# Second feed-forward of a hybrid block: up products of 20 tiles in pairs with seven block products for eight

## The chip, the cores and the metric

One core of a Trainium2 chip runs the kernel in one launch. The metric is the device time of an execution in microseconds. TensorE (PE) does the matmuls, VectorE (DVE) and ScalarE (ACT) the arithmetic on tiles, GpSimd (POOL) prepares weights, and SyncE (SP) issues the weight loads.

## The reference

What is computed, with one layer, 1024 tokens, a width of 1024 and D_FF = 2816, all in float32:

```python
def swiglu(h, w1, w3, w2):
    return (jax.nn.silu(h @ w1) * (h @ w3)) @ w2

def reference(...):
    ...
        h = modulate(rms_norm(x, g_ffn1[l]), sh1, sc1)
        x = x + 0.5 * gt1[:, None, :] * swiglu(h, w1_a[l], w3_a[l], w2_a[l])
        h = modulate(rms_norm(x, g_mix[l]), sh2, sc2)
        x = x + gt2[:, None, :] * hybrid_mixer(...)
        h = modulate(rms_norm(x, g_ffn2[l]), sh3, sc3)
        x = x + 0.5 * gt3[:, None, :] * swiglu(h, w1_b[l], w3_b[l], w2_b[l])
    return rms_norm(x, g_final)
```

The change is in the last `swiglu` alone, and in the order and the tiles of the norm ahead of it.

## The kernel before

Everything is held transposed: channels on the 128 partitions, the 1024 tokens along a row. A width of 1024 is 8 k tiles, D_FF is 22 f tiles. PSUM is four units of 128x1024 (`unit_a` to `unit_d`), each of two banks of 512 tokens.

**Split operands.** A float32 product is made of three fp32r matmuls, high by high, high by low and low by high (`product`, L486): each operand is split in a high part (a rounding copy) and a low part (the rest). One slab is one weight tile column, 8 k tiles of 128x128; a product of a slab with all tokens is 8 k tiles x 3 parts x 2 halves = 48 matmuls of 128x512. POOL splits the weights, half a slab (4 k tiles, 128x512) at a time: L456 makes `w_high`, L458 `w_low`. Two slabs of split weights are held, four of unsplit ones (`raw`), which SP loads ahead.

**Feed-forward.** The 22 f tiles go in chunks of 8, 8 and 6 (`CHUNKS`). `up`: the slab of w1 into unit_a, that of w3 into unit_b; ACT takes silu of unit_a (L840), DVE multiplies by unit_b (L1153), ACT makes `g_high` (L842) and DVE `g_low` (L1155). `down`, after each chunk: 8 output tiles, in unit_c and unit_d by turns, of 8 or 6 k tiles each; DVE adds each into the residual `x_res` (L1174). The very first pair of slabs (`first_pair`, L565) goes half by half of the tokens, k by k, right behind the norm; DVE makes the norm's `xr` (L1105) and `h_low` (L1113), ACT what is between (L830, L832). The last down chunk (`last_down`) is followed tile by tile by the end of the kernel: DVE scales with the final gain (L1187), PE transposes (L629), ACT squares (L776), DVE sums the squares (L1050).

The order on each engine is as written; engines meet by counting semaphores, and a wait holds up all that is behind it on its engine.

```python
for part in range(2):
    ...
    pool.wait_ge((slab_half, slab_used)[part], 4 * i + r - 1)
    high = w_high[:, r % 2, rows, :]
    pool.tensor_tensor(high, raw[:, r, rows, :], one, ALU.mult).then_inc(high_split, 1)
    pool.wait_ge(high_split, 2 * (4 * i + r) + part + 1)
    pool.tensor_tensor(w_low[:, r % 2, rows, :], raw[:, r, rows, :], high.bitcast(F32),
                       ALU.subtract).then_inc(slab_split, 1)
```

Of the kernel before, what the change touches and what calls it, by code (L numbers as in the profile page):

```python
# [30 lines left out]
P = 128  # L31
# [26 lines left out]
def phases():  # L58
# [17 lines left out]
    ffn("ffn2", False)  # L76
    out.append(("end", 0, (0, 0, 0, 0), 0, 0))
    return out

# [53 lines left out]
def block_kernel(nc, a, out):  # L133
    at = starts()
    with ExitStack() as ctx:
# [27 lines left out]

        x_rows = sb("x_rows", [P, J, D], rH)
# [34 lines left out]
        y_gain = sb("y_gain", [P, 2, T], rA)  # L199
        rms = sb("rms", [P, J], rA + 8 * KB)  # L200
# [108 lines left out]
        stored = sem("stored")  # L309
        act_step = sem("act_step")  # L310
        dve_step = sem("dve_step")

        block = ctx.enter_context(nc.Block())


        @block.sync
        def _(sp):
# [106 lines left out]
            ffn("ffn2", a["w1_b"][0], a["w3_b"][0], a["w2_b"][0], False)  # L424
# [12 lines left out]
        def _(pool):  # L437
# [24 lines left out]
            with pool.Fori(1, at["end"].slab // 4) as i:  # L462
                split(i, False)


        @block.tensor
        def _(pe):
# [164 lines left out]
            def last_down(i, count):  # L632

                here = at["ffn2.down2"]
                for e in range(2):
                    slab(here.slab + 2 * i + e, e, C_ + e, here.unit[C_ + e] + i, g_high, g_low, count,
                         (g_ready, here.g - count))
                    if e == 1:
                        back(2 * i, i, 0)
                    elif not isinstance(i, int):  # L640
                        back(2 * i - 1, i - 1, 1)

            def ffn(name, with_ada):
                for n, (_, count) in enumerate(CHUNKS):
# [4 lines left out]
                    if name == "ffn2" and n == 2:  # L649
                        last_down(0, count)  # L650
                        with pe.Fori(1, KD // 2) as i:
                            last_down(i, count)
                        back(KD - 1, KD // 2 - 1, 1)
                    else:
                        downs(f"{name}.down{n}", count, 1 if n == 2 else None)
# [96 lines left out]
            ffn("ffn2", False)  # L752
# [13 lines left out]
        def _(act):  # L766
# [36 lines left out]
            def norm(n, h0):  # L803
# [14 lines left out]
                for step in range(2 * KD):  # L818
# [4 lines left out]
                    half, m = divmod(step, KD)  # L823
                    t = slice(HALF * half, HALF * half + HALF)
                    tile = xr[n][:, step % 4, :]
# [6 lines left out]
                    act.activation(h_high[:, m, t], tile, ACT.Copy).then_inc(h_split, 1)  # L832
# [176 lines left out]
            norm(2, at["norm2"].h)  # L1009
            for n in range(3):  # L1010
                up("ffn2", n)
            here, ends = at["ffn2.down2"], at["end"]
            with act.Fori(0, KD // 2) as i:
                for e in range(2):
                    m = 2 * i + e
# [513 lines left out]
```

## Time and profile before

| | us |
|---|---|
| median of 3 executions (2393.04 to 2394.76) | 2393.91 |
| span of the profiled execution (first to last instruction) | 2389.7 |
| PE busy in it | 2308.2 (97%) |
| POOL busy in it | 1100.9 (46%) |
| DVE, ACT busy in it | 909.8 (38%), 320.6 (13%) |
| second feed-forward, from the first matmul to the last down tile | 1639.7 to 2369.2 |

The profiled execution has no time of its own beside its span; the span is 4.2 us under the median, which is taken as what lies around it. Times inside the profile are counted from its start. PE's busy time is drawn from modelled ends of pipelined matmuls, so the pace of a stretch is better read from the chain that ended last, where each piece is a run of matmuls with its length.

### The profile page before, as it was taken

The numbers are of one execution on the slowest core, as the hardware profiler recorded it, in microseconds if no ns is written. First come the engines' busy times: TensorE is split into PE (matmuls) and PEld (weight loads), VectorE is DVE, ScalarE is ACT, GpSimd is POOL, SyncE is SP. The second block draws the span as 40 slices with busy tenths as digits, with TensorE's granted clock in tenths as the row PEclk, the third lists the DMA queues.
The fourth block names the chain that finished last, engine by engine and source line by source line (L and its number), as shares of the span: only waits on it lengthen the run. The fifth ranks groups of instructions, "written<-read, shape, count | busy, mean of one in ns | idle before, by whom it ended". The sixth has DMA issues, their size and how long they took to land.

```text
span 2389.7 us, 27721 instructions
## 1 busy us (share of the span) xinstructions
PE 2308.2 (97%) x10370; PEld 1898.9 (79%) x10370; DVE 909.8 (38%) x1219; ACT 320.6 (13%) x372; POOL 1100.9 (46%) x824
## 2 busy tenths in 40 slices
PE   5899999999999899999999989999999999999997
PEld 4788788878888678888888867887888888888886
DVE  6645124331012699475665544436011101110134
ACT  3311000000011331010101121115110001000112
POOL 3354444444445453444444455543544444444452
PEclk8999999999999999999999999999999999999998
DMA  7344124321121332223222144411111111111111
GB/s 282 106 147 133 44 85 117 114 79 47 50 47 50 115 97 75 84 80 88 84 75 88 53 167 132 137 47 36 53 49 48 48 49 47 50 46 51 41 39 70
DMA packets 258446, 194.29 MB, mean 81 GB/s; under 512 B 21524, under 2 KB 238752, under 8 KB 257248
## 3 DMA queue, kind: packets, MB, share of 16 engines
q1 hardware_dynamic: 234752, 154.52, 21.3%
q10 hardware_dynamic: 23648, 39.20, 5.2%
q8 instruction: 24, 0.39, 0.1%
q14 instruction: 22, 0.18, 0.0%
HBM read 167.34 MB, written 25.17 MB: 81 GB/s over the span
## 4 chain that ended last, share of the span: by engine, by line
PE 93%; DVE 3%; ACT 1%; SPq 1%; issue 0%; DMA 0%; POOL 0%; DVEq 0%; POOLq 0%; ACTq 0%
PE unit_a L486 32%; PE unit_b L486 31%; PE unit_c L486 12%; PE unit_d L486 12%; PE unit_d L726 1%; PE unit_a L565 1%; SPq L340 1%; PE unit_b L565 1%; DVE xr L1105 1%; PE unit_c L609 1%; DVE rstd L1062 1%; PE unit_c L711 1%; PE unit_d L701 1%; PE unit_d L724 1%; PE unit_c L522 0%
## 5 line engine op out<-in xcount | busy, mean ns | idle before, releaser
L456 POOL TENSOR_TENSOR w_high<-raw,ones 128x512 fp32r<-128x512 f32 x408 | 545.3, 1336 | 1220.1 <-PE unit_b L486 395.7
L458 POOL TENSOR_TENSOR w_low<-raw,w_high 128x512 fp32r<-128x512 f32 x408 | 555.8, 1362 | 32.0
L486 PE MATMUL unit_a<-h_high,w_high 128*128 128x512 f32 x1072 | 333.7, 393 | 6.0 <-POOL w_low L458 4.7
L486 PE MATMUL unit_a<-h_low,w_high 128*128 128x512 f32 x1072 | 331.2, 390 | 0.0
L486 PE MATMUL unit_a<-h_high,w_low 128*128 128x512 f32 x1072 | 331.0, 390 | 0.0
L486 PE MATMUL unit_b<-h_high,w_high 128*128 128x512 f32 x1072 | 330.5, 389 | 0.0
L486 PE MATMUL unit_b<-h_high,w_low 128*128 128x512 f32 x1072 | 330.1, 389 | 0.0
L486 PE MATMUL unit_b<-h_low,w_high 128*128 128x512 f32 x1072 | 330.0, 389 | 0.0
L1153 DVE TENSOR_TENSOR s<-s,unit_b 128x1024 f32<-128x1024 f32 x44 | 53.7, 1221 | 655.5 <-PE unit_b L486 652.9
L486 PEld LDWEIGHTS unit_a<-h_high,w_high 128*128 128x128 f32 x1072 | 200.6, 189 | 48.4 <-POOL w_low L458 5.1
L486 PEld LDWEIGHTS unit_a<-h_low,w_high 128*128 128x128 f32 x1072 | 202.0, 188 | 42.5
L486 PEld LDWEIGHTS unit_a<-h_high,w_low 128*128 128x128 f32 x1072 | 201.8, 188 | 42.4
L486 PEld LDWEIGHTS unit_b<-h_low,w_high 128*128 128x128 f32 x1072 | 201.2, 188 | 41.9
L486 PEld LDWEIGHTS unit_b<-h_high,w_low 128*128 128x128 f32 x1072 | 201.2, 188 | 41.8
L486 PEld LDWEIGHTS unit_b<-h_high,w_high 128*128 128x128 f32 x1072 | 200.9, 188 | 42.0
L840 ACT ACTIVATE s<-unit_a 128x1024 f32<-128x1024 f32 x44 | 45.3, 1029 | 717.5 <-PE unit_a L486 712.6
L486 PE MATMUL unit_c<-g_high,w_high 128*128 128x512 f32 x388 | 121.0, 393 | 7.3 <-DVE mod L1160 7.3
L486 PE MATMUL unit_c<-g_low,w_high 128*128 128x512 f32 x388 | 120.7, 393 | 0.0
L486 PE MATMUL unit_c<-g_high,w_low 128*128 128x512 f32 x388 | 120.4, 392 | 0.0
L486 PE MATMUL unit_d<-g_high,w_high 128*128 128x512 f32 x388 | 119.7, 390 | 0.0
L486 PE MATMUL unit_d<-g_low,w_high 128*128 128x512 f32 x388 | 119.5, 389 | 0.0
L486 PE MATMUL unit_d<-g_high,w_low 128*128 128x512 f32 x388 | 119.5, 389 | 0.0
(233 smaller groups left out, 2266.0 us busy)
## 6 DMA issues: line engine op xcount, KB each, us to landing
raw<-in_w_a SPq DMA_DIRECT2D x60, 512.0 KB, 4.1
raw<-in_w_b SPq DMA_DIRECT2D x60, 512.0 KB, 3.8
raw<-in_w_in SPq DMA_DIRECT2D x44, 512.0 KB, 3.9
ada_raw<-in_w_ada SPq DMA_DIRECT2D x8, 2048.0 KB, 7.9
ada_raw<-in_w_ada SPq DMA_DIRECT2D x8, 1536.0 KB, 7.0
ada_first<-in_w_ada SPq DMA_DIRECT2D x8, 1024.0 KB, 14.2
sg_kept<-s ACTq DMA_DIRECT2D x16, 512.0 KB, 2.6
s<-sg_kept ACTq DMA_DIRECT2D x16, 512.0 KB, 3.3
```

The source lines that it names most:

```text
L340: sp.dma_start(raw[:, r, :, :], w.rearrange("(k p) (f n) -> p k f n", p=P, n=P)[:, :, 0, :]).then_inc(slab_loaded[r], 16)
L456: pool.tensor_tensor(high, raw[:, r, rows, :], one, ALU.mult).then_inc(high_split, 1)
L458: pool.tensor_tensor(w_low[:, r % 2, rows, :], raw[:, r, rows, :], high.bitcast(F32), ALU.subtract).then_inc(slab_split, 1)
L486: last = pe.matmul(unit[u][:, t], w, x[:, k, t], start=(k == 0 and part == 0), stop=(k == kts - 1 and part == 2))
L565: last = pe.matmul(unit[u][:, t], w, x[:, k, t], start=(k == 0 and part == 0), stop=(k == KD - 1 and part == 2))
L609: last = pe.matmul(unit[u][:, t], w, x[:, k, t], start=(k == 0 and part == 0), stop=(k == kts - 1 and part == 2))
L701: last = pe.matmul(unit[D_][0:H, col:col + P], b_now[rows, kk, part, :], ca[rows, kk, part, 0:8, :].rearrange("p d h -> p (d h)"), start=( ...
L711: last = pe.matmul(unit[C_][NS * g2:NS * g2 + NS, col:col + P], xt[:, kk, part, NS * g2:NS * g2 + NS], u_chunk[:, 2 * kk + g2, :], start=T ...
L724: pe.matmul(dst, toep[:, 4 * g2 + kk, :], u_chunk[:, 2 * kk + g2, :], start=True, stop=False)
L726: last = pe.matmul(dst, ca[rows, kk, part, 1:9, :].rearrange("p d h -> p (d h)"), sc_b[rows, kk, part, PAD:], start=False, stop=(part == 1))
L840: act.activation(s0[:, :], unit[A_][:, :], ACT.Silu).then_inc(unit_free[A_], 1)
L1153: dve.tensor_tensor(s1[:, :], s0[:, :], unit[B_][:, :], mul).then_inc(unit_free[B_], 1)
```

## The change

The first two f tiles are done as whole tiles, as before. The other 20 go in 10 pairs of f tiles, two pairs to a chunk, so five chunks. For a pair, w1 (and then w3) is a matrix of 2x2 blocks: rows are the two f tiles, columns the two halves of the 8 k tiles; the activations are 2x2 blocks too: halves of the k tiles by halves of the tokens. The product is made by the Winograd form of Strassen's method: seven block products, each of 4 k tiles x 3 parts = 12 matmuls of 128x512, in place of eight (a tile pair took 2 x 48 = 96 matmuls for a matrix, now 84). For this

- the four activation sums t1 to t4 (each 128x2048) are made once, by DVE, and split by ACT and DVE;
- each matrix needs four sums of weight blocks (128x512), made by POOL, and seven operands split: the high parts now by ACT, the low parts by POOL; `w_high` and `w_low` are a ring of four operands of 4 k tiles;
- the partial results of the four banks are put together by ACT (one copy) and DVE (adds), then silu, product and split of the result block by block: 128x512.

The down products come in six parts: two f tiles after the first pair's first matrix, then four f tiles after each chunk, 8 output tiles each time.

```diff
+PRODUCTS = (("a11", "b11", 0, True), ("s2", "t2", 1, True), ("s1", "t1", 2, True), ("s3", "t3", 3, True),
+            ("a12", "b21", 0, False), ("s4", "b22", 2, False), ("a22", "t4", 3, False))
...
 (POOL)
+            for o in range(8):
+                z, part = divmod(o, 2)
+                pool.wait_ge(w_loaded[z], 16)
+                if o < 4:
+                    pool.wait_ge((slab_half, slab_used)[part], s0_ - 1 + z)
+                else:
+                    pool.wait_ge(operand_used, o - 3)
+                whole(*operand(o % 4), o, raw[:, z, part * HK:(part + 1) * HK, :], one)
...
+            def matrix(here, n):
...
+                def low(q):
+                    pool.wait_ge(operand_high, N7 * m + q + 1)
+                    high, low_ = operand((RING[n] + q) % 4)
+                    pool.tensor_tensor(low_, weight_plain(PRODUCTS[q][0], slots), high.bitcast(F32),
+                                       ALU.subtract).then_inc(operand_low, 1)
+                    pool.wait_ge(operand_low, o + q + 1)
+
+                mixed = w_mixed[:, :, :]
+                summed(a_["a21"], a_["a11"], a_["a21"], ALU.subtract, 1)
+                summed(mixed, a_["a22"], a_["a21"], ALU.subtract, 2)
+                low(0)
+                summed(a_["a11"], mixed, a_["a11"], ALU.add, 3)
+                low(1)
+                summed(mixed, a_["a12"], mixed, ALU.subtract, 4)
+                for q in range(2, N7):
+                    low(q)
...
 (PE)
+            def tile_down(here, m):
...
+                take(C_ + e, at["ffn2"].unit[C_ + e] + here.uses + m // 2)
+                if m < 2:
+                    pe.wait_ge(evacuated, 14 * here.pair[1] + (10, 13)[e])
...
+            def whole_tiles():
...
+                    for n, k in enumerate((range(KD), SECOND_ORDER)[half]):
...
+                                if half == 1 and n == KD - 1 and (u, part) in ((A_, 1), (A_, 2), (B_, 1), (B_, 2)):
+                                    last.then_inc(operand_used, 1)
+                for e in range(2):
+                    take(C_ + e, here.unit[C_ + e])
+                    for k in range(KD):
+                        if k % HK == 0:
+                            pe.wait_ge(operand_low, 4 + 2 * e + k // HK + 1)
...
+            def banks_free(here, n):
+                pair = here.pair[n // 2]
+                if n % 2 == 1 and n // 2 == 0:
+                    for u in (C_, D_):
+                        take(u, at["ffn2"].unit[u] + here.uses)
...
+            def matrix(here, n):
...
+                banks_free(here, n)
+                for q, (_, b_name, to, anew) in enumerate(PRODUCTS):
+                    pe.wait_ge(operand_low, o + q + 1)
+                    if isinstance(o, int) and o == 8 and q in (1, 2, 3, 6):
+                        pe.wait_ge(act_sum_low, {1: 1, 2: 2, 3: 3, 6: 4}[q])
+                    if not anew and to == 0:
+                        pe.wait_ge(first_copied, here.matrix[n] + 1)
+                    elif not anew:
+                        pe.wait_ge(evacuated, done + to)
+                    wh, wl = operand((RING[n] + q) % 4)
+                    bh, bl = act_operand[b_name]
+                    for k in range(HK):
+                        for part, (w_, x) in enumerate(((wh, bh), (wh, bl), (wl, bh))):
+                            last = pe.matmul(bank(w, to), w_[:, k, :], x[:, k, :], ...)
+                    last.then_inc(operand_used, 1)
...
+            def fast_ffn():
+                whole_tiles()
+                here = Chunk(1)
+                matrix(here, 0)
+                first_down()
+                for n in range(1, 4):
+                    matrix(here, n)
+                for m in range(KD):
+                    tile_down(here, m)
+                with pe.Fori(2, PAIRED) as c:
...
-            ffn("ffn2", False)
+            fast_ffn()
...
 (ACT)
+            def weight_high(here, n, q):
...
+                act.wait_ge(operand_used, here.op[n] + q - 3)
+                act.activation(operand((RING[n] + q) % 4)[0], weight_plain(PRODUCTS[q][0], slots),
+                               ACT.Copy).then_inc(operand_high, 1)
...
 (DVE)
+            def act_sums():
+                plain = {name: x[:, :, :] for name, x in act_plain.items()}
+                for n, (to, x, y) in enumerate((("t1", "t3", "t1"), ("t3", "t2", "t3"), ("t2", "t2", "t1"), ("t4", "t4", "t2"))):
+                    dve.tensor_tensor(plain[to], plain[x], plain[y], sub).then_inc(act_sum, 1)
+                    dve.wait_ge(act_sum, n + 1)
...
+            act_sums()
+            sum_low("t2", 1)
+            sum_low("t1", 2)
+            sum_low("t3", 3)
+            whole_product(0)
+            sum_low("t4", 4)
+            whole_product(1)
```

In each matrix DVE adds a bank into an SBUF block five times; after the second matrix of a pair it also multiplies four blocks (one straight from PSUM, three with both factors in SBUF) and makes four low parts (both inputs in SBUF).

Three places in the order. **DVE, behind the norm ahead of the second feed-forward.** Before:

```order
L1113 TENSOR_TENSOR h_low<-xr_69,h_high 128x512 [waits h_split] x3
L1145 UNCONDITIONAL_BRANCH [waits h_ready]
L1145 ISA
L1152 ISA [waits unit_free_a]
L1153 TENSOR_TENSOR s_58<-s_57,unit_b 128x1024 [waits slab_used]
L1154 REGISTER_ALU
L1155 ISA [waits g_split]
L1155 TENSOR_TENSOR g_low<-s_58,g_high 128x1024
```

and in the changed kernel:

```order
L1560 TENSOR_TENSOR b_low<-t_plain,b_high 128x512 [waits h_split] x3
L1944 TENSOR_TENSOR t_plain<-t_plain 128x2048 [waits h_ready]
L1944 TENSOR_TENSOR t_plain<-t_plain 128x2048 [waits act_sum] x3
L1950 TENSOR_TENSOR t_low<-t_plain,t_high 128x2048 [waits act_sum_high,act_sum]
L1950 TENSOR_TENSOR t_low<-t_plain,t_high 128x2048 [waits act_sum_high] x2
L1955 TENSOR_TENSOR fg_two<-fg_two,unit_b 128x1024 [waits operand_used,silu_done]
L1950 TENSOR_TENSOR t_low<-t_plain,t_high 128x2048 [waits act_sum_high]
L1955 TENSOR_TENSOR fg_two<-fg_two,unit_d 128x1024 [waits operand_used,silu_done]
L1960 TENSOR_TENSOR fg_low<-fg_two,fg_high 128x1024 [waits fg_split] x2
```

Eight operations on 128x2048 have come in between the norm and the first results.

**POOL, from the second whole tile to the first matrix** (before, the loop of `split` goes on, two rows for half a slab):

```order
L628 TENSOR_TENSOR w_high<-raw,ones 128x512 [waits operand_used,w_loaded3]
L630 TENSOR_TENSOR w_low<-raw,w_high 128x512 [waits whole_high]
L650 TENSOR_TENSOR raw<-raw 128x512 [waits w_loaded1,w_loaded0]
L650 TENSOR_TENSOR w_mixed<-raw 128x512 [waits w_sum]
L656 TENSOR_TENSOR w_low<-raw,w_high 128x512 [waits operand_high,w_sum]
L650 TENSOR_TENSOR raw<-w_mixed,raw 128x512 [waits operand_low]
L656 TENSOR_TENSOR w_low<-w_mixed,w_high 128x512 [waits operand_high,w_sum]
L650 TENSOR_TENSOR w_mixed<-raw,w_mixed 128x512 [waits operand_low]
L656 TENSOR_TENSOR w_low<-raw,w_high 128x512 [waits operand_high,w_sum]
L656 TENSOR_TENSOR w_low<-raw,w_high 128x512 [waits operand_high,operand_low] x2
L656 TENSOR_TENSOR w_low<-w_mixed,w_high 128x512 [waits operand_high,operand_low]
L656 TENSOR_TENSOR w_low<-raw,w_high 128x512 [waits operand_high,operand_low]
```

The high parts have left POOL, and four sums have come: 11 operations for a matrix.

**ACT, behind the norm** (before: one silu of 128x1024 and one `g_high` for each f tile):

```order
L1364 ACTIVATE fg_two<-unit_a 128x1024 [waits operand_used]
L1378 ACTIVATE t_high<-t_plain 128x2048 [waits silu_done,act_sum]
L1378 ACTIVATE t_high<-t_plain 128x2048 [waits act_sum] x2
L1388 ACTIVATE w_high<-raw 128x512 [waits operand_used,w_loaded0]
L1388 ACTIVATE w_high<-w_mixed 128x512 [waits operand_used,w_sum]
L1378 ACTIVATE t_high<-t_plain 128x2048 [waits act_sum]
L1364 ACTIVATE fg_two<-unit_c 128x1024 [waits operand_used]
L1388 ACTIVATE w_high<-raw 128x512 [waits silu_done,operand_used,w_sum]
L1388 ACTIVATE w_high<-raw 128x512 [waits operand_used,w_sum]
L1374 ACTIVATE fg_high<-fg_two 128x1024 [waits unit_free_b]
L1374 ACTIVATE fg_high<-fg_two 128x1024 [waits unit_free_d]
L1388 ACTIVATE w_high<-raw 128x512 [waits operand_used]
```

The high parts of the weights now stand in one queue with the high parts of the sums and with the silus.

## Rows read from the trace of the kernel before

**Rows 1.** The page of the whole kernel: span, and busy time of each engine.
```profile
span 2389.7 us, 27721 instructions
...
PE 2308.2 (97%) x10370; PEld 1898.9 (79%) x10370; DVE 909.8 (38%) x1219; ACT 320.6 (13%) x372; POOL 1100.9 (46%) x824
```

**Rows 2.** The chain that ended last: start us, length us, engine, tile, line, count.
```profile
1667.09 11.22 PE unit_a L486 x48
...
2287.59 10.88 PE unit_b L486 x48
...
2298.47 8.16 PE unit_c L486 x36
```

**Rows 3.** Groups by shape, 1667 to 2390 us: busy us, mean ns | idle.
```profile
L458 POOL TENSOR_TENSOR w_low<-raw,w_high 128x512 fp32r<-128x512 f32 x131 | 169.9, 1297 | 10.3
...
L456 POOL TENSOR_TENSOR w_high<-raw,ones 128x512 fp32r<-128x512 f32 x131 | 169.2, 1292 | 340.5 <-PE unit_b L486 116.8 <-PE unit_a L486 112.0 <-PE unit_d L486 54.9
...
L1153 DVE TENSOR_TENSOR s<-s,unit_b 128x1024 f32<-128x1024 f32 x22 | 26.9, 1221 | 384.7 <-PE unit_b L486 382.2 <-ACT s L840 2.6
...
L842 ACT ACTIVATE g_high<-s 128x1024 f32 x22 | 23.3, 1061 | 236.6 <-DVE s L1153 236.6
...
L1174 DVE SCALAR_TENSOR_TENSOR x_res<-unit_c,gate,x_res 128x1024 f32 x8 | 10.3, 1284 | 72.0 <-PE unit_c L486 72.0
...
L776 ACT ACTIVATE s<-x_res 128x512 f32 x16 | 10.1, 632 | 57.6 <-DVE x_res L1179 57.4
...
L1050 DVE TENSOR_TENSOR s<-s,s 128x512 f32<-128x512 f32 x14 | 9.6, 686 | 0.6
...
L1179 DVE SCALAR_TENSOR_TENSOR x_res<-unit_d,gate,x_res 128x512 f32 x4 | 2.8, 747 | 6.4 <-PE unit_d L486 6.4
...
L1187 DVE TENSOR_SCALAR y_gain<-x_res,vt 128x1024 f32 x4 | 5.6, 1390 | 1.2 <-DVE x_res L1179 1.2
```

**Rows 4.** Timeline of DVE, 0 to 60 us: start, length, instruction.
```profile
21.27 9.80 DVE L1075 SCALAR_TENSOR_TENSOR ada_first_sum<-ada_first,cond,ada_first_sum 128x2048 f32<-128x2048 f32 x4 [1.19 <-DMA ada_first<-in_w_ada]
...
38.56 5.73 DVE L1075 SCALAR_TENSOR_TENSOR ada_first_sum<-ada_first,cond,ada_first_sum 128x2048 f32<-128x2048 f32 x2 [0.81 <-DMA ada_first<-in_w_ada]
...
44.21 5.09 DVE L1105 TENSOR_TENSOR xr<-x_res,rstd 128x512 f32<-128x512 f32 x3
```

**Rows 5.** Timeline of POOL in the same stretch.
```profile
35.69 3.19 POOL L458 TENSOR_TENSOR w_low<-raw,w_high 128x512 fp32r<-128x512 f32 x1
...
38.84 3.31 POOL L456 TENSOR_TENSOR w_high<-raw,ones 128x512 fp32r<-128x512 f32 x1
```

**Rows 6.** Timeline of DVE, 1618 to 1700 us.
```profile
1663.25 1.36 DVE L1113 TENSOR_TENSOR h_low<-xr,h_high 128x512 fp32r<-128x512 f32 x1 [0.34 <-ACT h_high L832]
...
1667.17 1.22 DVE L1153 TENSOR_TENSOR s<-s,unit_b 128x1024 f32<-128x1024 f32 x1 [2.56 <-ACT s L840]
...
1669.75 1.29 DVE L1155 TENSOR_TENSOR g_low<-s,g_high 128x1024 f32 x1 [1.35 <-ACT g_high L842]
```

**Rows 7.** Timeline of POOL, 1618 to 1700 us.
```profile
1668.67 1.29 POOL L456 TENSOR_TENSOR w_high<-raw,ones 128x512 fp32r<-128x512 f32 x1
...
1670.04 2.15 POOL L458 TENSOR_TENSOR w_low<-raw,w_high 128x512 fp32r<-128x512 f32 x1
```

**Rows 8.** The chain, 1640 to 1680 us: end of the first pair.
```profile
1665.29 0.69 PE unit_a L565 x3
...
1666.01 1.04 ACT s L840
```

**Rows 9.** PE alone in windows of 2 us: busy us, granted clock, DMA.
```profile
1378.00:1380.00 2.00, 0.78 (x2) 0.83 0.69 242
...
1380.00:1382.00 2.00, 2.00 (x6) 0.50 0.98 270
```

**Rows 10.** Timeline of ACT, 1618 to 1700 us: the norm's last operation.
```profile
1662.59 0.63 ACT L832 ACTIVATE h_high<-xr 128x512 fp32r<-128x512 f32 x1
```

**Rows 11.** The chain: the 24 matmuls behind a gap of PE.
```profile
1379.22 7.30 PE unit_a L486 x24
```

More of the change, by code:

```diff
@@ L461, in _, with whole @@
             split(0, True)
[L462 removed]
+            with pool.Fori(1, at["ffn2"].slab // 4) as i:
                 split(i, False)
+            two_by_two = ones[:, :].rearrange("p (a b n) -> p a b n", a=1, b=1).to_broadcast([P, 2, 2, P])
+            def whole(high, low, n, plain, by):
+                pool.tensor_tensor(high, plain, by, ALU.mult).then_inc(whole_high, 1)
+                pool.wait_ge(whole_high, n + 1)
+                pool.tensor_tensor(low, plain, high.bitcast(F32), ALU.subtract).then_inc(operand_low, 1)
@@ L466, in _ @@
+            for n in range(1, 4):
+                matrix(here, n)
+            down(here)
+            with pool.Fori(2, PAIRED + 1) as c:
+                here = Chunk(c)
+                for n in range(4):
+                    matrix(here, n)
+                down(here)
         @block.tensor
@@ L630, in back @@
                 last.then_inc(out_full, 1)
[L632 to L641, printed above, removed]
+            def tile_down(here, m):
+                e = m % 2
+                pe.wait_ge(operand_low, here.down_op + m + 1)
+                take(C_ + e, at["ffn2"].unit[C_ + e] + here.uses + m // 2)
+                if m < 2:
+                    pe.wait_ge(evacuated, 14 * here.pair[1] + (10, 13)[e])
+                wh, wl = operand(m % 4)
+                for k in range(4):
+                    pe.wait_ge(fg_ready, 2 + 4 * here.pair[k // 2] + 3 + k % 2)
+                    for part, (w, x) in enumerate(((wh, fg_high), (wh, fg_low), (wl, fg_high))):
+                        for half in range(2):
+                            t = slice(HALF * half, HALF * half + HALF)
+                            last = pe.matmul(unit[C_ + e][:, t], w[:, k, :], x[:, k, t], start=(k == 0 and part == 0),
+                                             stop=(k == 3 and part == 2))
+                last.then_inc(operand_used, 1)
             def ffn(name, with_ada):
@@ new lines, in matrix @@
+            def matrix(here, n):
+                o, w = here.op[n], n % 2
+                done = 14 * here.pair[n // 2] + 5 * w
+                banks_free(here, n)
[11 more added lines that the diff above has]
+                        for part, (w_, x) in enumerate(((wh, bh), (wh, bl), (wl, bh))):
+                            last = pe.matmul(bank(w, to), w_[:, k, :], x[:, k, :],
+                                             start=(anew and k == 0 and part == 0),
+                                             stop=(k == HK - 1 and part == 2), skip_group_check=True)
+                    last.then_inc(operand_used, 1)
@@ new lines, in _ @@
+            for which in range(4):
+                pair_silu(here, 0, which)
+            matrix(here, 1, after=False)
+            for n in (2, 3):
+                matrix(here, n)
+            for which in range(4):
+                pair_high(here, 3, which)
+            with act.Fori(2, PAIRED + 1) as c:
+                here = Chunk(c)
+                for n in range(4):
+                    matrix(here, n)
+                for which in range(4):
+                    pair_high(here, 3, which)
@@ L1013, in _ @@
+            ends = at["end"]
             with act.Fori(0, KD // 2) as i:
@@ L1498, in _ @@
+            here = Chunk(PAIRED)
+            for n in range(4):
+                matrix(here, n)
+            clear_sums(3)
+            down(None, gate[1][:, :], 3, used=operand_used, first=here.down_op)
             dve.wait_ge(root_done, 7)
```

402 lines of the change are left out of this document (367 added, 35 removed).

## Prediction

> **What bounds the kernel now.** I read the page first: PE is busy for 2308 of 2390 us, POOL for less than half [rows 1]. A busy PE may still be a waiting one, so the next view is the chain that ended last, for the second feed-forward. It is nothing but matmuls [rows 2]: a slab of 48 takes 10.88 us, 0.2267 us each, a pace that holds at the last slab 620 us later, and in the down tiles of 36 (8.16 us). No gap shows where one slab ends and the next, with waits of its own, begins. So this stretch costs its number of matmuls times 0.2267 us. The groups of the stretch [rows 3] show what the other engines need: a half-slab operation of POOL takes 1.29 us, and POOL waits for PE for 340 us; everything there is cover.
>
> The profiled execution spans 2389.7 us and the median of the runs is 2393.9, 4.2 more. The sum is made on the span's rows and I add those 4.2 again at the end. A measurement of this kernel can tell about 0.2% (4.8 us) from no change.
>
> **Matmuls.** Before, up: 44 slabs x 48 = 2112. Now: 4 slabs of whole tiles x 48 = 192, and 20 matrices x 7 products x 12 = 1680. Down is 1056 both times (before 8 x (48+48+36); now 8 x 12 + 5 x 8 x 24). So 240 matmuls go, and 240 x 0.2267 = **54.4 us** leave the chain. Each matmul had a weight load of its own before and has one now, so the price of one stays.
>
> **Is the rest fed in time?** A product lasts 12 x 0.2267 = 2.72 us, a matrix 19.04 us. Per matrix:
> - POOL: 4 sums and 7 low parts. Rows 7 show consecutive starts 1.37 us apart, so 11 x 1.37 = 15.1 us: inside 19.04, but no longer with half its time free.
> - ACT: for a pair of matrices 14 high parts, 2 copies, 4 silus, 4 high parts of results, 24 operations on 128x512. A square of that size takes 0.63 us [rows 3], so 15.1 us of 38.1.
> - DVE: 10 adds out of PSUM, 4 products, 4 low parts. An addition of 128x512 takes 0.69 us [rows 3]: 12.4 us of 38.1.
>
> Latency counts too. The ring holds four operands, so the operand of product q may be filled once product q-4 has ended, 3 products (8.16 us) before it is wanted; filling is one ACT copy and one POOL operation, about 2.1 us. The tight place is the start of a matrix, where POOL does 4 sums and 3 low parts in a row. The last low part of the matrix before is done 2.1 us after its third product; 7 x 1.37 = 9.6 us later, at 11.7, the third operand is ready, and its product begins at 6 x 2.72 = 16.3. That is 4.6 us of slack. Adds out of PSUM stay ahead too: bank 0 must be copied by the fifth product, and its copy is due 1.3 us after the first ends, 8.2 before it is wanted; banks 2 and 3 have 5.4 us for two or three adds of 0.7. From a chunk's last matrix to the down part, the last product, low parts and multiply take some 2.9 us, while PE has 4.1 us of other k tiles to do. Loads: two slabs for 19 us, each landing in some 4 us, is near the pace of before. So in 20 matrices and 40 later down tiles I take **0 us** lost. If this cover is gone, every product pays; that is rival C.
>
> **DVE against POOL.** One thing is new: DVE now works on two SBUF inputs beside a much busier POOL. What that costs is seen at the kernel's start. DVE's 128x2048 operation takes 2.4 us when POOL is idle (9.80 for four) [rows 4]. Beside it POOL's 1.3 us operation takes 3.19 and 3.31 us [rows 5]: one POOL operation is done for each DVE one, about 1.1 us after that ends, and DVE's two take 5.73, its next three of 128x512 5.09 (1.7 each instead of 0.69). A POOL operation beside one DVE operation of 128x1024 with both inputs in SBUF takes 2.15 us [rows 6, 7]; one beside DVE's read of unit_b (at 1667.17) keeps its 1.29. Inside the matrices this is 7 small operations per pair, at most 7 x 0.4 = 3 us of POOL's 8 us to spare: nothing on the path.
>
> **The start, where it does count.** The norm's last ACT operation ends at 1663.2 [rows 10], and DVE's last low part, 1.36 us beside POOL before [rows 6], can end at 1664.0 without it, since POOL now has nothing to do there. Then DVE starts four sums and, behind them, four low parts of 128x2048, about 2.3 us each. The first pair of slabs ends on PE at 1665.98 (unit_a) and 1666.67 (unit_b) [rows 8]. Before, POOL had split the next half slab by then. Now all four operands are released only by the pair's last six matmuls, so POOL starts at 1665.8, behind DVE's first sum, which ends at 1666.3. From there both alternate with 3.2 us a turn: POOL's operations end at 1667.4, 1670.6, 1673.8, 1677.0, 1680.2, 1683.4. Two are wanted for each operand. PE can start unit_c at 1670.6, its second half at 1677.0, unit_d at 1683.4, and ends unit_d 10.88 later, at 1694.3. Before, this second tile ended at 1667.09 + 11.22 + 10.88 = 1689.19 [rows 2]. That is **5.1 us lost**. DVE has work for these turns: the highs of t2, t1, t3 from ACT, 1.9 us each (0.63 for 512 columns and 1.06 for 1024 [rows 3], so 0.43 for each 512 more), are ready at 1674.6, 1676.6 and 1678.5, before DVE wants them.
>
> The pause of 4 us before unit_c may also cost clock. After the gap that ends at 1379.22 the granted clock is 0.50 (1.2 GHz) [rows 9], and 24 matmuls take 7.30 us in place of 5.44 [rows 11], 1.9 us more. Here this falls on the first half of unit_c: 1670.6 + 5.4 + 1.9 = 1677.9, and PE would have waited until 1677.0 anyway; unit_d still starts about 1683.4. So it is 0 in the sum, up to 2 in the range.
>
> [...]
>
> The first matrix: POOL goes on with the last operand (done 1687.9), two sums and low part 0 at 1692.0, before PE wants it at 1694.3. DVE's product of the first tile, which frees unit_b, is done by 1687. The later operands come 0.5 to 2 us before their products, by the same turns. 0 us, up to 3 in the range.
>
> One more wait is new: matrix 1 of the first chunk needs unit_c and unit_d, which the first down part uses last; DVE's add of its last tile takes 1.28 us [rows 3] and PE waits for it, with hand-over **1.4 us**. In later chunks a matrix on unit_a and unit_b stands between.
>
> **The end.** The last down tiles shrink from 36 to 24 matmuls, 5.44 us, with 0.87 of transposes 6.3 in place of 9.05. DVE's work for one is two adds of 0.75, y_gain's 1.39 and two sums of 0.69 [rows 3], with half a copy of unit_b (1.2, as L1153) about 5 us: it still fits. What follows the last tile, some 20 us, is untouched.
>
> **Sum.** -54.4 + 5.1 + 1.4 = -47.9. 2389.7 becomes 2341.8, and with the 4.2 around it **2346.0**.
>
> **The rivals.**
> A. The forecast: 0.62, with a range of its own from 2343 to 2352.
> B. The start is free: DVE's sums don't hold POOL, or POOL gets in first. Then unit_c starts two POOL operations after 1665.8, at 1668.5, and unit_d ends at 1690.3, 1.1 us late: 2342.0. For it: DVE's operation of 1.29 us at 1669.75 wasn't held up itself [rows 6], so who comes first matters, and POOL may come first. Against it: [rows 5]. 0.10.
> C. Each of the 140 products pays a little at its start for two or three waits on PE. For it: a product has fewer matmuls than a slab to hide them, and the first slab of the stretch took 11.22. Against it: the down slabs wait at every k tile and keep 8.16 for 36. Bounds are 0 and 0.34 us a product (nothing excludes a little gain either, but no row shows one); at 0.1 it is 14 us: 2360. 0.20.
> D. The other side: POOL becomes the bound inside the matrices. It decides there once 11 operations take longer than a matrix by what the change gains, 19.04 + 47.9/20 = 21.4 us, or 1.95 us an operation. Beside DVE a turn took 1.7 (128x512) or 2.15 (128x1024). If DVE's 9 or 13 operations per matrix, those that read PSUM too, held POOL to 2.15, a matrix would take 23.7 us and the kernel 2346 + 20 x 4.6 = 2438. Against it: DVE is busy for a third of the time and the reads of PSUM didn't touch POOL. 0.06.
> E. It isn't what it says: the products would not be 12 matmuls, or whole tiles stay. The order shows 84 matmuls a matrix; 0.02, near 2394.
>
> **The numbers.** The time is that of A, 2346.0. The range must reach below for B with its own spread (2339), and above over A's upper end and the better part of C, up to 0.14 us a product (2346 + 20 = 2366); D, E and the rest of C are left out. Faster by over 0.2%: A, B, C: 0.92. Within: 0.03, E and the edge between C and D. Slower: 0.05.
>
> **What would show it.** In the chain of waits the products appear as runs of 12 at 2.72 us, with no POOL between them; unit_c starts near 1670.6 and unit_d ends near 1694; PE waits about 1.4 us for DVE's add once, near 1735. POOL's operations beside the 128x2048 ones take 3.2 us, elsewhere 1.3 to 1.7, with about 60 to 85% busy in the matrices. Wrong it would be if runs of 12 take over 2.8 us, if PE waits for low parts or for adds out of banks within a chunk, or if the span from unit_c's start to the last down tile isn't shorter by about 50 us.

## The result and the profile after

| | before | after |
|---|---|---|
| median of the runs, us | 2393.47 (4 runs) | 2367.91 (2365.88 to 2368.49, 4 runs) |
| ratio, 95% interval | | 0.989 [0.9876, 0.9904] |
| span of the profiled execution, us | 2389.7 | 2366.9 |

The change gains 25.6 us; 47.9 were forecast, and 2367.9 lies above the range (2339 to 2366). The sign was right, the size was not.

The page of the changed kernel, against [rows 1]: 240 matmuls fewer on PE, and more work on all the others.

```profile
span 2366.9 us, 28072 instructions
...
PE 2267.9 (96%) x10130; PEld 1863.1 (79%) x10130; DVE 1087.4 (46%) x1391; ACT 419.1 (18%) x569; POOL 1199.0 (51%) x876
```

PE lost 40 us of busy time, not 54, so even its busy time holds something new. PE's waits from 1600 to 2370 us (line waited for, us in total, times, longest) say where to look:

```profile
PE unit_c L875 <- DVE fg_low L1987: 10.8, 5, 2.2
...
PE unit_c L925 <- POOL w_low L630: 4.2, 1, 4.2
PE unit_c L963 <- issue: 1.4, 1, 1.4
PE unit_b L963 <- POOL w_low L656: 0.9, 1, 0.9
```

The second to fourth are the start and the 1.4 us that were forecast, with a remainder. The first, the largest, was not forecast at all: it comes once in each chunk, where the down part begins. The chain there, at the end of the second chunk (start, length, what):

```profile
1917.30 2.73 PE unit_d L963 x12
...
1920.06 0.70 DVE fg_one L1977
...
1924.11 0.69 DVE fg_one L1977
1924.82 1.07 DVE fg_two L1983
1925.88 1.68 DVE fg_low L1987
...
1927.61 4.62 PE unit_c L875 x12
1932.23 5.44 PE unit_d L875 x24
```

Twelve matmuls behind the wait take 4.62 us in place of 2.72, and the next 24 have their old 5.44. In the other four chunks the first twelve take 4.28, 3.03, 4.61 and 3.06 us, and one run of 24 takes 5.82. That is 1.56 + 1.90 + 0.31 + 1.89 + 0.34 + 0.38 = 6.4 us. The granted clock shows what most of it is. PE in windows of 2 us at the end of the first chunk, where twelve took 4.28 (busy times, with the clock third from the end):

```profile
1804.00:1806.00 2.00, 2.00 (x8) 1.61 (x9) 0.39 (x1) 0.00 (x0) 0.00 (x0) 0.82 0.63 174
1806.00:1808.00 2.00, 2.00 (x6) 1.52 (x6) 0.00 (x0) 0.00 (x0) 0.00 (x0) 0.50 0.29 88
1808.00:1810.00 2.00, 2.00 (x9) 1.61 (x8) 1.28 (x1) 0.00 (x0) 1.65 (x2) 0.83 0.00 0
1810.00:1812.00 2.00, 2.00 (x11) 1.63 (x10) 0.00 (x0) 0.00 (x0) 0.93 (x1) 1.00 0.00 0
```

PE had waited for some 2 us until 1803.84. The clock then falls to 0.50, the lower of the two levels (1.2 GHz), and is back at 1.00 (2.4 GHz) by 1810. At the second and the fourth chunk's end it falls as well (0.54 from 1928 to 1930, 0.50 from 2174 to 2176). At the third and the fifth it does not, as the same view shows for the third:

```profile
2052.00:2054.00 2.00, 2.00 (x11) 1.61 (x9) 0.00 (x0) 0.00 (x0) 0.00 (x0) 1.00 0.82 242
```

There the first twelve take 3.03 and 3.06 us at a granted clock of 1.00: a restart costs 0.3 us of its own. So the five chunk ends cost 10.8 us of waits and 6.4 us of slow matmuls behind them (5.7 where the clock fell, 0.65 where it did not), **17.2 us**.

Whole spans are a blunt measure for what follows: this one had reached the end of the first pair of second-feed-forward tiles 2.7 us later than before. That is jitter and not the change: the changed kernel and those of the experiments reach this point between 1666.7 and 1669.3. I therefore use **the stretch**: from the end of the last matmul into unit_b of that pair to the end of the last down tile. Before it runs from 1666.67 to 2369.22, 702.5 us; after from 1669.34 to 2343.86, 674.5 us. The forecast for it was 702.5 - 47.9 = 654.6. The missing 19.9 us are the 17.2 of the chunk ends, 2.4 more at the start, and 0.3 of small pieces.

The start, in the chain: POOL's turns, and the third product of the first matrix behind them.

```profile
1670.16 3.19 POOL w_low L630
1673.35 3.30 POOL w_high L628
...
1676.73 3.22 POOL w_low L630
...
1696.66 3.24 POOL w_low L656
...
1699.97 2.24 POOL w_mixed L650
...
1702.29 2.14 POOL w_low L656
...
1704.48 5.74 PE unit_b L963 x24
```

Behind the stretch another 2.4 us went. It went in the 32 small matmuls of the closing statistics, from 0.8 us after the last transposes on (the chain):

```profile
2347.69 0.22 PE unit_c L1113 x2
2347.92 0.23 PE unit_c L1114 x2
2348.14 0.43 PE unit_c L1113 x2
2348.57 0.43 PE unit_c L1114 x2
...
2352.84 0.44 PE unit_c L1114 x2
```

A pair goes from 0.22 to 0.43 us, at a granted clock of 0.50 from 2349 to 2353. From the last tile to the end of the statistics, 2343.86 to 2353.28 is 9.4 us, before it was 7.0. So -28.0 + 2.4 = -25.6, which is what the medians show.

### The profile page after: what moved, and what is told of

Read it like the earlier page. It is cut to its first block, busy times and chain, and to the rows that moved or that the text cites. A ratio compares the mean times of both kernels' runs of the same rounds, so it can differ in the third digit from the quotient of the medians.

```text
span 2366.9 us, 28072 instructions
## 1 busy us (share of the span) xinstructions
PE 2267.9 (96%) x10130; PEld 1863.1 (79%) x10130; DVE 1087.4 (46%) x1391; ACT 419.1 (18%) x569; POOL 1199.0 (51%) x876
## 4 chain that ended last, share of the span: by engine, by line
PE 90%; DVE 5%; POOL 2%; ACT 1%; issue 1%; DMA 0%; SPq 0%; DVEq 0%; POOLq 0%; ACTq 0%
PE unit_a L715 22%; PE unit_b L715 22%; PE unit_c L715 7%; PE unit_d L715 7%; PE unit_d L875 5%; PE unit_b L963 5%; PE unit_c L875 4%; PE unit_d L963 4%; PE unit_c L963 3%; PE unit_a L963 3%; PE unit_d L1079 1%; DVE rstd L1510 1%; PE unit_c L838 1%; DVE fg_low L1987 1%; PE unit_c L1064 1%
## 5 line engine op out<-in xcount | busy, mean ns | idle before, releaser
L615 POOL TENSOR_TENSOR w_high<-raw,ones 128x512 fp32r<-128x512 f32 x272 | 370.2, 1361 | 847.8 <-PE unit_a L715 280.3
L715 PE MATMUL unit_a<-h_high,w_high 128*128 128x512 f32 x736 | 230.2, 394 | 5.5 <-POOL w_low L617 4.7
L715 PE MATMUL unit_a<-h_low,w_high 128*128 128x512 f32 x736 | 227.9, 391 | 0.0
L715 PE MATMUL unit_a<-h_high,w_low 128*128 128x512 f32 x736 | 227.7, 390 | 0.0
L715 PE MATMUL unit_b<-h_high,w_high 128*128 128x512 f32 x736 | 227.0, 390 | 0.0
L715 PE MATMUL unit_b<-h_high,w_low 128*128 128x512 f32 x736 | 226.7, 389 | 0.0
L715 PE MATMUL unit_b<-h_low,w_high 128*128 128x512 f32 x736 | 226.5, 389 | 0.0
L656 POOL TENSOR_TENSOR w_low<-raw,w_high 128x512 fp32r<-128x512 f32 x100 | 135.1, 1351 | 90.2 <-ACT w_high L1388 82.9
L715 PEld LDWEIGHTS unit_a<-h_high,w_low 128*128 128x128 f32 x736 | 138.7, 188 | 29.3
L715 PEld LDWEIGHTS unit_b<-h_low,w_high 128*128 128x128 f32 x736 | 138.2, 188 | 28.6
L628 POOL TENSOR_TENSOR w_high<-raw,ones 128x512 fp32r<-128x512 f32 x52 | 76.5, 1472 | 111.6 <-PE unit_c L875 38.0
L1388 ACT ACTIVATE w_high<-raw 128x512 fp32r<-128x512 f32 x100 | 63.3, 633 | 312.3 <-PE unit_c L875 127.6
L1523 DVE SCALAR_TENSOR_TENSOR ada_sum<-ada_raw,cond,ada_sum 128x512 f32<-128x512 f32 (+1 forms) x112 | 111.0, 991 | 4.0
```

Of the source, the lines that this page charges most:

```text
L628: pool.tensor_tensor(high, plain, by, ALU.mult).then_inc(whole_high, 1)
L656: pool.tensor_tensor(low_, weight_plain(PRODUCTS[q][0], slots), high.bitcast(F32), ALU.subtract).then_inc(operand_low, 1)
L715: last = pe.matmul(unit[u][:, t], w, x[:, k, t], start=(k == 0 and part == 0), stop=(k == kts - 1 and part == 2))
L1388: act.activation(operand((RING[n] + q) % 4)[0], weight_plain(PRODUCTS[q][0], slots), ACT.Copy).then_inc(operand_high, 1)
L1523: last = dve.scalar_tensor_tensor(out=dst[:, 0:count], in0=src[:, k, 0:count], scalar=by, in1=dst[:, 0:count], op0=mul, op1=add)
```

## Experiments

**The theory.** At a chunk's end DVE owes PE a chain of sums and low parts. POOL splits the operands of the down tiles just then, with inputs in SBUF like DVE's, and the two take turns, so that DVE's operations with both inputs in SBUF take 1.1 to 1.8 us in place of 0.69. Here are both beside each other at the second chunk's end, DVE first (start, length, instruction, idle before). The last product ends on PE at 1922.74.

```profile
1920.06 0.69 DVE L1977 TENSOR_TENSOR fg_one<-fg_one,unit_d 128x512 f32<-128x512 f32 x1 [0.52 <-PE unit_d L963]
1920.78 1.70 DVE L1983 TENSOR_TENSOR fg_two<-fg_two,fg_one 128x512 f32<-128x512 f32 x1
1922.41 1.78 DVE L1987 TENSOR_TENSOR fg_low<-fg_two,fg_high 128x512 fp32r<-128x512 f32 x1
1924.11 0.68 DVE L1977 TENSOR_TENSOR fg_one<-fg_one,unit_d 128x512 f32<-128x512 f32 x1
1924.82 1.07 DVE L1983 TENSOR_TENSOR fg_two<-fg_two,fg_one 128x512 f32<-128x512 f32 x1
1925.81 2.35 DVE L1987 TENSOR_TENSOR fg_low<-fg_two,fg_high 128x512 fp32r<-128x512 f32 x2
```
```profile
1920.66 1.27 POOL L628 TENSOR_TENSOR w_high<-raw,ones 128x512 fp32r<-128x512 f32 x1
1922.01 1.62 POOL L630 TENSOR_TENSOR w_low<-raw,w_high 128x512 fp32r<-128x512 f32 x1
1923.59 1.74 POOL L628 TENSOR_TENSOR w_high<-raw,ones 128x512 fp32r<-128x512 f32 x1
```

The add that reads unit_d in PSUM keeps its 0.69; the two behind it, with both inputs in SBUF, don't. The last add could start at 1922.8 and starts at 1924.11, because DVE is still at the low part before. The last line holds the third and the fourth low part. PE's wait ends at 1927.61 with the third, which k tile 2 needs; in DVE's order it stands behind the last product's add and multiply, although it belongs to the product before. The rivals: DVE is late by the length of its chain, whoever works beside it; or the wait is one of order, and PE has work it could do first.

In the table and below, "stretch" is the one defined above; its change against the changed kernel is the cleaner number, since neither the jitter ahead of it nor the clock of the closing statistics is in it. The differences are taken before rounding. Medians of before in these runs were 2393.5 to 2394.1.

| run | median, us | ratio to before | stretch, us | against after |
|---|---|---|---|---|
| after | 2367.9 | 0.989 [0.9876, 0.9904] | 674.5 | |
| hold POOL | 2349.3 | 0.982 [0.9803, 0.9836] | 657.3 | -17.2 |
| two tiles interleaved | 2349.7 | 0.9819 [0.9802, 0.9835] | 658.2 | -16.3 |
| early release | 2362.6 | 0.9871 [0.9855, 0.9888] | 672.3 | -2.2 |
| late unit_d | 2364.7 | 0.988 [0.9863, 0.9896] | 671.1 | -3.5 |
| small operations at the start | 2372.6 | 0.9913 [0.9896, 0.993] | 678.1 | +3.5 |
| POOL 13 a matrix | 2364.1 | 0.9877 [0.986, 0.9893] | 671.3 | -3.3 |
| POOL 15 a matrix | 2374.3 | 0.992 [0.9904, 0.9937] | 683.0 | +8.5 |
| two tiles + early + late | 2345.3 | 0.98 [0.9784, 0.9817] | 654.5 | -20.1 |
| hold + early + late | 2347.2 | 0.9805 [0.9792, 0.9819] | 653.6 | -20.9 |
| all four | 2346.1 | 0.9801 [0.9788, 0.9814] | 654.5 | -20.0 |

### Hold POOL at the chunk's end

```diff
 # POOL, down(), before operand n
+if n == 2:
+    pool.wait_ge(fg_ready, 2 + 4 * here.pair[1] + 4)
```

> The changed kernel with one wait more: ahead of the third of a chunk's eight down operands POOL waits until DVE has made the chunk's last low part. Theory 1 (DVE is late at the end of a chunk because each of its two-SBUF-input operations takes turns with POOL, 1.7 us in place of 0.7): POOL is quiet from about the sixth product on, the multiply and the low parts run at 0.7 us, PE's five waits for fg_low (10.8 us together) and the clock lost behind them (6.4 us) go: 2351, and at most one wait of under 0.5 us is left a chunk. Theory 2 (the latency of the chain of hand-overs between DVE and ACT is too long even at full pace): the waits keep more than half of their length, 2362 or over. Theory 3 (POOL's split is what the down part waits for): the hold makes it worse, over 2368.

2349.28 us. The line with the waits for fg_low is gone. DVE at the same place, and the chain of PE:

```profile
1914.54 0.69 DVE L1985 TENSOR_TENSOR fg_two<-fg_two,fg_one 128x512 f32<-128x512 f32 x1
1915.14 0.68 DVE L1989 TENSOR_TENSOR fg_low<-fg_two,fg_high 128x512 fp32r<-128x512 f32 x1
...
1917.26 0.69 DVE L1985 TENSOR_TENSOR fg_two<-fg_two,fg_one 128x512 f32<-128x512 f32 x1
1917.86 1.48 DVE L1989 TENSOR_TENSOR fg_low<-fg_two,fg_high 128x512 fp32r<-128x512 f32 x2
```
```profile
1911.96 4.53 PE unit_d L965 x20
1916.50 5.44 PE unit_c L877 x24
1921.94 4.08 PE unit_d L877 x18
```

With POOL silent the operations are back at 0.7, and no gap stands in the down tile behind the last product. That product ends at 1916.50 and the third low part some 2.1 us later, inside the 2.72 us of PE's other k tiles. Nothing else was changed, so DVE's chain isn't too long in itself: POOL beside it is the cause. The stretch shrinks by 17.2, the waits and the slow matmuls behind them together.

### Interleave the first two down tiles

PE does k tiles 0 and 1 of both tiles first, then 2 and 3 of both; POOL is left alone.

```diff
-for m in range(KD):
+two_downs(here)        # k tiles 0, 1 of unit_c and unit_d, then 2, 3 of both
+for m in range(2, KD):
     tile_down(here, m)
```

> The changed kernel, but PE does the first two down tiles of a chunk in turns: k tiles 0 and 1 of both, then k tiles 2 and 3 of both. POOL and DVE work as before. Theory 1 and theory 2 both say that the last low part comes some 5 us after the last product; PE now has 5.44 us of work that doesn't need it, in place of 2.72: the waits of 2.2 us go and with them the lower clock, 2351. If the loss at the end of a chunk had nothing to do with these low parts (the wait for unit_d or for POOL's operands), the time stays at 2365 to 2368, with a wait of PE for DVE's fg_one or for POOL in its place.

2349.68 us. DVE is as slow as before (fg_low 1560 ns in the mean), and the waits are gone all the same, but for two of 0.6 us or less: PE has 5.44 us of work where it had 2.72. So the loss can be cured at either end. A third way was not tried: an order on DVE in which the third low part does not stand behind the last product's operations.

### Release one of the first pair's operands early

The pair's half slabs come in their natural order, and the first of the four operands is given back at half of the k loop.

```diff
-SECOND_ORDER = (0, 4, 1, 5, 2, 6, 3, 7)
+SECOND_ORDER = (0, 1, 2, 3, 4, 5, 6, 7)
...
-if half == 1 and n == KD - 1 and (u, part) in ((A_, 1), (A_, 2), (B_, 1), (B_, 2)):
+if half == 1 and (n, u, part) in ((HK - 1, A_, 2), (KD - 1, A_, 2), (KD - 1, B_, 1), (KD - 1, B_, 2)):
```

> The changed kernel with the second half of the tokens in the first pair done in the natural order of k tiles, and the first operand released at k tile 3 of it instead of at the end. POOL can split the next operand before DVE's sums of 128x2048 begin. Theory (start): unit_c starts right behind the first pair, the 4.2 us wait goes; POOL's later operations still take 3.2 us turns, so the end of unit_d comes 3 to 5 us sooner: 2363 to 2365. If instead the number of POOL turns up to the first matrix sets the time, and not when they start, it is the same as before within 1 us (2367 to 2368).

2362.63 us. The wait of 4.2 us before unit_c is gone, but smaller ones stand in its place:

```profile
PE unit_a L963 <- POOL w_low L656: 2.0, 2, 1.6
...
PE unit_b L963 <- POOL w_low L656: 1.5, 1, 1.5
PE unit_c L963 <- issue: 1.4, 1, 1.4
PE unit_d L925 <- POOL w_low L630: 1.4, 2, 0.8
```

(The 1.4 before unit_c is the old wait for unit_d at matrix 1.) POOL has the same turns with DVE to get through, so the waits only moved: 4.9 us in sum, where the changed kernel had 5.1. What the stretch gained, 2.2 us, is the lower clock: no wait is as long as 4.2 us any more, the granted clock stays at 1.00 from 1670 to 1710, and the 2.7 us of slow matmuls behind the long wait are gone, less some 0.3 for a restart. The late release was a part of the start's loss; the turns are the rest. (The median fell by 5.3; the closing statistics ran at 0.22 us a pair here for most of their length, some 2 us of it.)

### Take unit_d later in matrix 1

```diff
-for u in (C_, D_):
-    take(u, at["ffn2"].unit[u] + here.uses)
+take(C_, at["ffn2"].unit[C_] + here.uses)
...
+if n == 1 and q == 2:
+    take(D_, at["ffn2"].unit[D_] + here.uses)
```

> The changed kernel, but the second matrix of the first chunk waits only for unit_c at its start, and for unit_d at its third product. Expected: PE's one pause of 1.4 us at 1740 goes and nothing else changes: 1.4 us less, 2366.5, at the edge of what three rounds tell; the profile has to show it.

2364.72 us. The wait of 1.4 us is gone: unit_c follows at 1739.87 directly on the last down tile. The stretch gained 3.5, more than that: the first twelve matmuls behind the five chunk-end waits, which were as long as ever (10.7 us), took 3.02, 4.61, 3.01, 4.61 and 3.02 us, and the run of 24 that took 5.82 is back at 5.44. That is 1.7 us less than in the changed kernel. Another 0.3 is the edit's own, since the 24 matmuls behind the vanished wait take 5.44 for 5.70. The 1.7 is chance or phase, and not the edit's doing as far as I can show.

### Cut the start's large DVE operations in four

Each 128x2048 operation of DVE's sums and low parts becomes four of 128x512.

> The changed kernel with DVE's four sums and four low parts of the activations cut in four instructions of 128x512 each. Lock theory: DVE and POOL take turns by instruction, so a turn is 1.7 us in place of 3.2: POOL's six operations for unit_c and unit_d take some 10 us in place of 19, unit_c starts about 1.5 us sooner and unit_d 5 us sooner; but DVE now needs up to 28 turns (up to 47 us, less once POOL is idle), and the product that frees unit_b and the low parts of t2 may come late: between 2363 and 2371. If the two shared the port by bandwidth and not by instruction, cutting would change nothing: POOL's operations would stay at 3.2 us.

2372.63 us, slower by 4.7, a little over what was expected. POOL did get quicker turns (1.6 to 1.7 us for 3.2), and PE waits 2.8 before unit_c for 4.2. But now DVE is the one left behind (DVE's timeline, then PE's waits from 1600 to 2300 us):

```profile
1665.17 20.62 DVE L1945 TENSOR_TENSOR t_plain<-t_plain 128x512 f32<-128x512 f32 x16
1685.83 13.86 DVE L1953 TENSOR_TENSOR t_low<-t_plain,t_high 128x512 fp32r<-128x512 f32 x12
```
```profile
PE unit_a L963 <- issue: 6.7, 1, 6.7
```

Sixteen sums take 20.6 us; the same sums as four took 12.1. PE stands 6.7 us before its first product, until 1700.9: DVE's low parts last until 1699.7, and the multiply that frees unit_b comes behind them. While POOL has work the turns are per instruction: whoever cuts its work into smaller pieces gets a smaller share.

### More work for POOL in the matrices

In every matrix the low part of two products (then four) is computed once more, into a tile that nobody reads there: 13 and 15 operations where there were 11.

```diff
+if q in (4, 6):              # second kernel: (3, 4, 5, 6)
+    pool.tensor_tensor(ada_sum..., weight_plain(PRODUCTS[q][0], slots), high.bitcast(F32), ALU.subtract)
```

> The changed kernel with two more POOL operations in each matrix (ahead of the low parts of the fifth and seventh operand, into a tile that nobody reads): 13 in place of 11. If the cover of POOL inside a matrix is what the sum said, 13 x 1.37 = 17.8 us still lie inside 19.04: no wait for low parts inside the matrices, 2367 to 2369; at the end of a chunk DVE may be a little later still.

> The same with four more POOL operations in each matrix (ahead of the low parts of the fourth to seventh operand): 15 x 1.37 = 20.6 us are 1.5 us longer than a matrix. If POOL's pace is the bound there, PE waits for low parts, in chunks partly made good by the down part, where POOL is half idle: 10 to 40 us more, 2378 to 2405. If it stays near 2368, POOL's operations are cheaper than their 1.37 us, and the rival of a POOL-bound matrix was further off than the sum said.

With 13 the time is 2364.08: nothing lost. (The stretch is even 3.3 shorter; the chunk-end waits are 9.5 us in place of 10.8, and fewer matmuls behind them are slow. That other operations of POOL meet DVE's now is my guess at the reason.) With 15 it is 2374.27, and PE waits for POOL inside the matrices of every chunk (waits from 1600 to 2300 us):

```profile
PE unit_c L966 <- POOL w_low L659: 5.0, 5, 1.3
...
PE unit_b L966 <- POOL w_low L659: 3.3, 9, 0.9
...
PE unit_c L878 <- DVE fg_low L1990: 3.2, 4, 0.9
```

POOL is busy for 79 to 89% of the time there. The stretch is 8.5 us longer, but that is a difference of two things. By PE's timeline the four matrices of a chunk take 80.2 to 80.4 us in place of 76.2 in the last four chunks, and 58.3 in place of 57.2 in the first: 17.7 us more, 1.0 us a matrix in the last 16. The rest got 9.2 us cheaper, since the waits for fg_low at the chunks' ends are 4.1 us over all five in place of 10.8, and with them went slow matmuls. A matrix at POOL's pace thus takes 20.1 us, 1.34 an operation, close to the 1.37 of the forecast. The expectation had 2378 at least and had not counted the cheaper chunk ends; why they got cheaper isn't shown. So the change stands two to four operations a matrix away from being bound by POOL: rival D wasn't near, and it doesn't explain the result.

### All cures together

> The three edits that undo the three losses together: first two down tiles in turns, first operand released early, unit_d waited for late. Theory: the losses are at three places and add up: 17.2 + 4.5 + 1.4 = 23 us less than the changed kernel, 2344 to 2345, 50 us under the kernel before. If they cover each other (a loss that goes shows up at the next wait), 2347 to 2350.

> The down-part hold of POOL (as in the first experiment), the early release of the first pair's operands and the late wait for unit_d together; PE takes the down tiles in their own order. If the three savings add (18.6 + 5.3 + 3.2 by their medians, the last of which by its wait is only 1.4), 2339 to 2343. If holding POOL costs something that interleaving the two tiles does not (POOL's operands for the next down tiles late), 2345 or more.

> The version with interleaved down tiles, early release and late wait for unit_d (2345.3 alone), and POOL held until DVE is done as well. Theory: both cures remove the same wait, so nothing is gained by the second: 2344 to 2347. Rival: interleaving leaves a remainder (DVE's turns still late for k tile 2), which the hold takes away: 2339 to 2343, and the same as the other run of this call.

Interleaved tiles, early release and late unit_d: 2345.3 us, near the 2344 to 2345 expected, and 0.98 [0.9784, 0.9817] of before. The hit is in part luck: the stretch gained 20.1 us, where 23 were expected, and the other 2.5 came behind it, where the closing statistics kept their clock. With POOL held in place of the interleaving 2347.2, and with both 2346.1. The three don't differ within their spread. The second was expected at 2339 to 2343, from a sum of medians. That was an error of method: the stretches are 654.5, 653.6 and 654.5 us, all 48 to 49 below before. The three medians had gained 27.1 us together, the three stretches 22.9: the difference lies outside the stretch. Of the 22.9, the 1.7 by which the kernel with unit_d taken late had faster matmuls at the chunk ends can't be had again once those waits are gone, which leaves 21.2, and 20.9 were measured. Holding and interleaving remove the same wait, so that the one on top of the other gains nothing. In the version with hold, early release and late unit_d, PE's clock and share in windows of 100 us show that nothing is left to gain by better feeding inside the chunks:

```profile
1800.00:1900.00 100.00, 100.00 (x443) 82.81 (x442) 31.04 (x31) 25.22 (x43) 67.65 (x52) 1.00 0.17 48
1900.00:2000.00 100.00, 100.00 (x442) 82.79 (x442) 37.74 (x39) 21.41 (x36) 64.77 (x49) 1.00 0.18 53
```

At the start something is left: there PE still waits 4.8 us for POOL in this version (2.0 and 1.5 for w_low at L656, 1.3 at L630). The stretch of 653.6 stands 5.5 us over 702.5 - 54.4 = 648.1, what the matmuls alone would give.

## Why the prediction was wrong

**The matmuls: right.** Products run in pieces of 12 at 2.72 us or of 24 at 5.44, without a gap inside a chunk; 54.4 us left the chain. That POOL, ACT and DVE keep up inside the matrices was right, as was rejecting rivals C and D: no product pays, and POOL has two operations a matrix to spare.

**The chunk's end: the step that failed.** The prediction said: "From a chunk's last matrix to the down part, the last product, low parts and multiply take some 2.9 us, while PE has 4.1 us of other k tiles to do." and took 0 us lost. Both numbers were wrong, and it is DVE's 2.9 that cost the time: with POOL held DVE took 2.1 us, and PE's 2.72 covered it.
- PE has 2.72 us, not 4.1: the first operations to be waited for are those of k tile 2, behind 12 matmuls, not those of k tile 3, behind 18. (The 4.1 would not have covered k tile 3 either: its low part ends at 1928.16, 5.4 us after the last product.)
- DVE takes 4.8 us from the last product's end at 1922.74 to the end of the third low part, the one that k tile 2 needs, near 1927.6. Three operations lie between, 2.1 us at 0.69 each; beside POOL they take 3.4. And DVE comes to the first of them 1.4 us late, since the multiply and the low part before were slowed in the same way.

I had seen this contention in the trace of before and priced it from one side, as the 3 us of POOL's time that small DVE operations could take. What POOL's operations do to DVE's wasn't asked, although [rows 4] showed three of 128x512 in 5.09 us. And the cover was set against durations of an engine that works alone. Each of the five ends lost 2.1 us of wait, and 6.4 us more went in slow matmuls behind the five waits, most of it to the clock: the working put a price on a wait of PE as its own length, except at the start.

**The start: mechanism right, size off.** The turns are 3.19 to 3.35 us, the forecast's 3.2. The Trainium skill (SBUF — State Buffer, Who interferes with whom) says that a VectorE instruction with two SBUF inputs contends with a GpSimd one that reads SBUF, since its second input comes through the shared read interface. The trace agrees: POOL's operation, 1.29 us alone, takes 3.19 to 3.35 beside DVE's 128x2048 ones. One strictly after the other, DVE's 2.4 and POOL's 1.3 would make 3.7 us; the turns stand 3.3 us apart, so some 0.4 us of the two overlap. unit_d's tile ends 28.6 us after the pair (1669.34 to 1697.96), where 27.6 were forecast. Half of the 1.0 is the turns, 3.3 in place of 3.2 five times over: POOL had unit_d's first operand ready 17.2 us after the pair, at 1686.54, where the forecast had 16.7. The other half is the clock: after the wait unit_c's 48 matmuls took 13.6 us in place of 10.9 (1673.50 to 1687.08), 2.7 more where the prediction had 1.9 and held that this would fall on time that PE waits anyway; most of it did. Then the third product of the first matrix waits for its low part, behind turns of 3.24, 2.24 and 2.14 us, and starts at 1704.48 in place of 1703.40; with 0.3 for the restart behind it, that is 1.4, where the forecast had operands that come 0.5 to 2 us early, 0 in the sum and up to 3 in the range. Together 7.5 for 5.1.

**The wait for unit_d at matrix 1: right**, 1.42 us for 1.4.

**The closing statistics: not considered.** "What follows the last tile, some 20 us, is untouched" held for the work and not for its clock: 2.4 us. Runs differ in this: the three with the interleaving kept 0.22 us a pair, the two with POOL held and no interleaving had 0.43 for most. What decides it I can't say.

**The sum.** -54.4 + 7.5 + 1.4 + 17.2 + 0.3 = -28.0 in the stretch, and +2.4 behind it: -25.6. With the chunk ends covered and nothing else changed the stretch is 657.3 (POOL held) or 658.2 (interleaved), against the 654.6 that were forecast; the 2.7 that the first leaves are the 2.4 of the start and 0.3 of small pieces. That all cures together give 654.5 is a coincidence: there the 1.4 us wait for unit_d, which the forecast counted as lost, is gone, and the start costs more than the forecast's 5.1. So rival A had the right mechanisms elsewhere, missed one wait, and sized the start too small. None of the rivals had that wait, and the range above was only as wide as C made it.

## What to carry to other kernels

When a change gives an engine that was idle more work, ask for both sides of every pair of engines that share SBUF: what the newcomer loses, and what it takes from the one that PE is going to wait for. Check the cover at the place where the pipeline drains (the end of a chunk), not only in its middle, and set it against durations measured with the neighbour at work. Then the smallest cure is one of order: let the engine that isn't urgent wait for the one that is, or give PE the independent half of two tiles first.

## What the runs showed that I had not expected

- A wait of PE costs more than its length, but not always the same: behind three of five waits of 2.1 to 2.2 us the granted clock fell to 0.50, and the next twelve matmuls took 4.28 to 4.62 us in place of 2.72. Behind the other two it read 1.00, and they took 3.03 and 3.06. The same 0.3 stands behind the shorter waits (24 matmuls in 5.74 behind 0.9 us, in 5.70 behind 1.4). In the kernel with unit_d taken late the same waits had 3.02, 4.61, 3.01, 4.61 and 3.02. What decides which wait lowers the clock is open.
- DVE and POOL, both with inputs in SBUF, alternate by instruction, not by bytes: with 128x2048 DVE needed 12.1 us for four sums, with 128x512 it needed 20.6 for the same, while POOL's turns fell from 3.2 to 1.7 us.
- Reads of PSUM by DVE stay at 0.68 to 0.69 us beside a busy POOL, all through the chunks (means of 680 to 689 ns by group).
